# Routed experts: the first gather ahead of the adding products, the first turn of rows inside the second expert's products

## The reference

```
def routed_experts(xt, e_idx, e_w, w_gate, w_up, w_down):
    ...
    def block_ffn(args):
        tok, wt, e = args
        xb = xt[tok]
        hb = jax.nn.silu(xb @ w_gate[e]) * (xb @ w_up[e])
        return (hb @ w_down[e]).astype(F32) * wt[:, None]
    ...
    return jnp.zeros((T, D), F32).at[row_tok].add(yb.reshape(rows, D))
```

## Time and profile before

| | |
|---|---|
| median of 3 runs | 1155.11 us (1152.92 to 1156.42) |
| the profiled execution, its own time | 1163.27 us |
| its span in the trace | 1160.6 us |
| mean granted TensorE clock in it | 0.968 of full |
| PE, DVE, ACT busy | 94%, 73%, 61% of the span |

### The profile page before, as it was taken

One profiled execution on the slowest core, in us unless ns is written; L12 is line 12 of the kernel. 1 busy time (PEld: TensorE's weight loads), 2 busy tenths in 40 slices (PEclk: granted clock), 3 DMA queues, 4 the chain that ended last, 5 costly groups with the idle time before them and its releaser, 6 DMA issues.

```text
span 1160.6 us, 17178 instructions
## 1 busy us (share of the span) xinstructions
PE 1088.2 (94%) x6358; PEld 941.4 (81%) x6358; DVE 843.7 (73%) x1086; ACT 713.5 (61%) x945; POOL 77.3 (7%) x82
## 2 busy tenths in 40 slices
PE   7999969999999999889999999999999878999997
PEld 6877857777877787669988899998788667999996
DVE  5497588999999999567654776667778646767665
ACT  6667359888888887464444555445467545544553
POOL 1001110000000000030000111020000001101100
PEclk9998879999999999889999999999999989999999
DMA  9440518888888888435553554554433223554440
GB/s 372 158 173 4 205 55 326 320 332 328 327 333 324 341 329 330 185 145 182 182 174 117 202 195 154 210 185 154 170 134 120 73 73 131 214 217 181 175 151 36
DMA packets 33605, 232.64 MB, mean 200 GB/s; under 512 B 3856, under 2 KB 3984, under 8 KB 6032
## 3 DMA queue, kind: packets, MB, share of 16 engines
q1 hardware_dynamic: 32688, 229.98, 53.5%
q10 hardware_dynamic: 864, 1.93, 0.5%
HBM read 230.85 MB, written 1.05 MB: 200 GB/s over the span
## 4 chain that ended last, share of the span: by engine, by line
PE 77%; DVE 13%; ACT 6%; issue 3%; POOL 1%; DMA 0%; DVEq 0%; ACTq 0%; POOLq 0%
PE bank L1834 11%; PE bank L1835 11%; PE bank L1836 11%; PE bank L2320 9%; PE bank L2322 9%; PE bank L2321 9%; DVE wlo L1092 5%; PE bank L2189 4%; PE bank L2190 4%; PE bank L2173 2%; ACT whi L512 1%; PE bank L2197 1%; PE bank L2238 1%; PE bank L2237 1%; DVE arena L1482 1%
## 5 line engine op out<-in xcount | busy, mean ns | idle before, releaser
L1092 DVE TENSOR_TENSOR wlo<-raw,whi 128x2048 fp32r<-128x2048 f32 x212 | 482.0, 2287 | 88.6 <-ACT whi L512 87.3
L512 ACT ACTIVATE whi<-raw 128x2048 fp32r<-128x2048 f32 x213 | 406.5, 1917 | 121.9 <-PE bank L2322 65.6
L2320 PE MATMUL bank<-xs,whi 128*128 128x256 f32 x896 | 252.0, 281 | 4.7 <-DVE wlo L1092 3.2
L2321 PE MATMUL bank<-xs,whi 128*128 128x256 f32 x896 | 251.3, 280 | 0.0
L2322 PE MATMUL bank<-xs,wlo 128*128 128x256 f32 x896 | 250.7, 280 | 0.0
L2320 PEld LDWEIGHTS bank<-xs,whi 128*128 128x128 f32 x896 | 169.4, 189 | 6.9 <-DVE wlo L1092 3.6
L2321 PEld LDWEIGHTS bank<-xs,whi 128*128 128x128 f32 x896 | 169.5, 189 | 0.8
L2322 PEld LDWEIGHTS bank<-xs,wlo 128*128 128x128 f32 x896 | 169.4, 189 | 0.0
L1834 PE MATMUL bank<-whi,rounded 128*128 128x512 f32 x344 | 142.2, 413 | 7.4 <-DVE rounded L1491 4.2
L1835 PE MATMUL bank<-wlo,rounded 128*128 128x512 f32 x344 | 139.5, 405 | 0.0
L1836 PE MATMUL bank<-whi,rounded 128*128 128x512 f32 x344 | 139.5, 405 | 0.0
(11 more groups left out here) (319 smaller groups left out, 1475.1 us busy)
## 6 DMA issues: line engine op xcount, KB each, us to landing
raw<-stream SPq DMA_DIRECT2D x215, 1024.0 KB, 4.8
arena<-finals ACTq DMA_DIRECT2D x3, 512.0 KB, 4.3
xres<-x_in SPq DMA_DIRECT2D x2, 512.0 KB, 4.6
raw<-stream SPq DMA_DIRECT2D x4, 256.0 KB, 6.1
out<-xn SPq DMA_DIRECT2D x4, 256.0 KB, 2.1
par<-params SPq DMA_DIRECT2D x1, 844.0 KB, 12.4
cst<-table SPq DMA_DIRECT2D x1, 502.0 KB, 8.9
arena<-p_in ACTq DMA_DIRECT2D x1, 256.0 KB, 5.7
```

Source lines behind the costliest of these rows:

```text
L512: act.activation(whi[:, s, :], raw[:, a, :], ACT.Copy).then_inc(S("high_done"), 1)
L1092: dve.tensor_tensor(wlo[:, s, :], raw[:, unit0 % RAW, :], whi[:, s, :].bitcast(F32), ALU.subtract)\
L2320: pe.matmul(o, whi[:, s, w], xhi[:, kk, :], start=first, stop=False, skip_group_check=True)
L2321: pe.matmul(o, whi[:, s, w], xlo[:, kk, :], start=False, stop=False, skip_group_check=True)
```

## The change

On PE, `fetch(0)` moves in front of `scatter`, with two waits ahead of it: that for `pick_ready`, which stood behind `scatter`, and a new one for the first half of `y_low`, since the gather writes bank 2. `turn_rows(x, 0)` moves from ahead of `pair_gate_up(x, 1)` to between its two units. On ACT, `out(0)` comes ahead of `ahead(4)`, `ahead(5)` ahead of `silu_pair(x, 0)`, `out(2)` ahead of `hidden_high(x, 0)`, and `back_out` goes to the end. On DVE, `pick_quad` and `quad_weights` move from the start of the pair to between `ahead(2)` and `ahead(3)`. No instruction is added or removed but waits.

```
# ACT
                 gate_up_out(x, 0)
+                out(0)
                 ahead(4)
-                out(0)
+                ahead(5)
                 silu_pair(x, 0)
-                ahead(5)
                 gate_up_out(x, 1)
                 out(1)
+                out(2)
                 hidden_high(x, 0)
-                out(2)
                 silu_pair(x, 1)
-                back_out(x)
                 out(3)
                 hidden_high(x, 1)
+                back_out(x)
...
# DVE
-                if not x.second and x.p0 and not x.last_quad:
-
-                    dve.wait_ge(S("slots_turned"), x.count(1))
-                    four = bass.ds(x.quads(1) * 4, 4)
-                    pick_quad(four, 1 - x.buf)
-                    quad_weights(four, 1 - x.buf, S("pick_ready"))
                 ahead(0)
                 ahead(1)
                 if x.p0:
                     y_low(x.count(2, -2))
                 ahead(2)
+                if not x.second and x.p0 and not x.last_quad:
+
+                    dve.wait_ge(S("slots_turned"), x.count(1))
+                    four = bass.ds(x.quads(1) * 4, 4)
+                    pick_quad(four, 1 - x.buf)
+                    quad_weights(four, 1 - x.buf, S("pick_ready"))
                 ahead(3)
...
# PE
                 pair_gate_up(x, 0)
+                if not x.second and not x.last_quad:
+                    pe.wait_ge(S("pick_ready"), x.quads(2))
+                if x.p0:
+
+                    pe.wait_ge(S("y_pair"), x.count(2, -1))
+                fetch(0)
                 if x.p0:
                     scatter(x.count(1))
-                if not x.second and not x.last_quad:
-                    pe.wait_ge(S("pick_ready"), x.quads(2))
-                fetch(0)
-                turn_rows(x, 0)
-                if x.p0:
-                    pe.wait_ge(S("summed"), x.count(2))
-                pair_gate_up(x, 1)
+                    pe.wait_ge(S("summed"), x.count(2))
+                pair_gate_up(x, 1, (0,))
+                turn_rows(x, 0)
+                pair_gate_up(x, 1, (1,))
                 fetch(1)
```

More of the change, by code:

```diff
@@ L1513, in pair_dve @@
                 ahead = (lambda k: split_to(U_MOE + 6 * x.p0 + k)) if x.j is None else (lambda k: split(x.unit(k)))
+                ahead(0)
+                ahead(1)
+                if x.p0:
+                    y_low(x.count(2, -2))
+                ahead(2)
                 if not x.second and x.p0 and not x.last_quad:
@@ L1519, in pair_dve @@
                     quad_weights(four, 1 - x.buf, S("pick_ready"))
-                ahead(0)
-                ahead(1)
-                if x.p0:
-                    y_low(x.count(2, -2))
-                ahead(2)
                 ahead(3)
@@ L2177, in gather, with pair_gate_up @@
                     ins.then_inc(S("gathered"), 1)
-            def pair_gate_up(x, e):
-                for i in range(2):
+            def pair_gate_up(x, e, units=range(2)):
+                for i in units:
                     if x.p0 == 0 and e == 0:
```

## The result

The changed kernel takes 1172.18 us in the median (1171.26 to 1174.32, 4 runs) against 1154.01 (1151.43 to 1156.42, 4 runs): the ratio is 1.016, with a 95% interval of 1.0132 to 1.0189. It is slower by 18 us, where 17.9 were forecast.

What follows compares the result with a forecast made beforehand. PE was taken to bound the expert stage, busy 37.26 of 38.0 us per quad. The terms 12.4 + 8.0 - 0.9 - 1.6 = +17.9 us on the median of 1155.11 gave 1173 us, +1.5%, range 1163 to 1180.

Steps and rivals of the forecast that it cites:

- The gap of 0.72 us at the first units goes: First expert's units on PE, pairs with a pick: 0.72 us less in six pairs, a gain of 4.3 us.
- t0: Start of the last down product of the pair before, from which the prediction counted each pair's times.
- The wait, +12.4 us: PE's gather waits for DVE's late pick, 2.6 us idle; six pairs together become 12.4 us longer.
- the 2.06 of the sum: Net lengthening in us of each pair with a pick, 6.75 - 4.69, with the first units' gain inside.
- The walk from t0: DVE's pick starts at t0 + 5.74, the gather at about t0 + 6.75; PE is there at t0 + 3.97.
- The clock, +8.0 us from five falls of 1.6: Idle 2.6 us ahead of the gather halves PE's clock in five of six pairs, 1.6 us each.
- The turn of rows and the earlier gather: nothing: PE's sum unchanged; DVE's first fold 0.83 us later, inside its 1.00 us idle ahead of the second fold.
- The last quad, -0.9 and -1.6 us: ACT's `gate_up_out` starts 0.45 us earlier in each of two pairs, -0.9; one of two clock falls may stay away, -1.6.
- wait without the clock: Rival: 2.6 us of idle leaves the clock alone, 12.4 - 0.9 - 1.6 = +9.9, 1165 us; chance 0.13.

Runs made afterwards that it cites:

- the filled wait: The changed kernel with 20 added products of 256 columns on PE ahead of the wait for the pick, against the kernel before: 1165.78 us, ratio 1.0077.
- half filled kernel: The changed kernel with 10 added products of 256 columns on PE ahead of the wait for the pick, against the kernel before: 1165.7 us, ratio 1.0091.

## Why the prediction was right

1. *The gap of 0.72 us at the first units goes.* Yes: after, the first units start at t0 + 0.24 (288.16) and 1.86 later (290.02), without a gap, and the gap is back with the pick first.
2. *The wait, +12.4 us.* Measured with the clock kept up, 240.41 - 228.05 = 12.4 us; each of the six pairs is 1.98 to 2.09 us longer, for the 2.06 of the sum. The walk from t0 along ACT, DVE and PE met each start of the pair shown within 0.1 us. Idle times were 2.49 to 2.60 for the 2.6 forecast, 15.2 us for 15.6.
3. *The clock, +8.0 us from five falls of 1.6.* The mechanism holds: filling the wait, wholly or by half, removes all falls. The size was somewhat high. A fall costs about 1.5 us (a pair with one takes 22.77 to 22.95 us, one without 21.4 to 21.5), and the two profiles of the changed kernel have 5 (counting the long one twice) and 3; the stretch of pairs 1 to 13 exceeds that with the filled wait by 247.86 - 240.41 = 7.5 us in one and 244.84 - 240.41 = 4.4 us in the other. By time, the difference of the ratios, 0.83% to 0.72%, is 8 to 10 us; the medians of the changed and the half filled kernel, timed side by side, differ by 6.4.
   Five falls in six rested on six idle times of over 2 us that had all brought one in a single profile. That was too little to go by. In the twelve profiles PE idles 1.88 to 3.64 us ahead of its first product behind the pairs (2.67 in the kernel before); a fall follows in eight of them, once after 1.88 us, and in four none does, once after 3.36 us (the kernel with the pick ahead of `y_low`; the slices are as for the changed kernel run again):

```profile
474.29 0.50 PE L1834 MATMUL bank<-whi,rounded 128*128 128x512 f32 x1 [3.36 <-DVE wlo L1092]
```

```profile
472.00:474.00 2.00, 0.00 (x0) 1.00 0.00 0
474.00:476.00 2.00, 1.71 (x7) 1.00 0.36 66
476.00:478.00 2.00, 2.00 (x14) 1.00 0.88 360
```

   So the length of one idle time does not decide, at these lengths; the share that falls does the pricing, and in the loop it was seven of twelve.
   The Trainium skill (TensorE: Matmul & The Clock Gate, section 'HAM oscillation — how this bites in real kernels') tells of a loop whose wait brings the clock down in every round. Its waits are longer than these, and no run here has such waits in its loop.
4. *The turn of rows and the earlier gather: nothing.* Nearly: with the pick first the pairs have their old lengths, but for the one that waited for a load. DVE's wait for the turned rows divides as expected: there it is 16.6 us in 30 times, where it was 18.6 in 16.
5. *The last quad, -0.9 and -1.6 us.* The order was worth 0.5, not 0.9: `gate_up_out` starts 0.4 us earlier (0.69 for 1.10), but 0.15 us of each pair does not come through. The clock gave up to twice the 1.6: with the new order none of nine profiles has a fall at the last quad's waits (0.69 and 0.65 us); with the old one (1.10 and 0.65 us) all three have one at pair 15's first down product, and the kernel before has one at pair 14's too. That is one or two falls avoided, 1.4 to 2.9 us.

The sum came out to 0.3 us of the measured medians. Its parts were +12.4, +4.4 to 7.5, -0.5 and -1.4 to -2.9, in all 13 to 18; the interval of the ratio is 15 to 22 us. So the closeness of the total is partly luck, that of the wait's term not. The rival 'wait without the clock' is what the two filled kernels are, and it measured 1.0077 and 1.0091, where it was priced at 1.0086 (9.9 of 1155).

Open is why a wait of the same length brings a fall in some rounds and not in others. Not run was the late pick with the early gather alone, without ACT's order and the later turn of rows; that these two have no part in the cost rests on the trace, where the gather waits for the pick's weights and nothing else, and on the walk.

## What to carry to other kernels

Where an instruction moves ahead on one engine and what it waits for moves back on another, walk both engines from one common event to the meeting point: here the late pick alone was free (0.9994), and so was the rest of the change without it (0.9969), but both together cost 1.6%. Look for the place of the producer that is early enough for its consumer and late enough not to hold up the first splits: ahead of `y_low` the pairs with a pick were 0.5 us shorter than before, behind it 0.4, and one split later still they were 2 us longer, and more where the clock fell. A recurring idle time of PE can have a second price, the clock's, and work that covers half of it removed that price wholly here. How often the clock falls cannot be read off a handful of idle times in one profile.

## What the runs showed of the hardware

Useless products made the kernel faster: 10 added products of 256 columns in each of six waits (which left 1.3 to 1.4 us idle of 2.5 to 2.6) took 0.7% off, by keeping the granted clock at 1.00 where it had fallen to 0.50. In the loop idle times of 1.3 to 1.4 us brought no fall in six cases, those of 2.5 to 2.6 us brought seven in twelve. No single length divides the two kinds: in the last quad 1.10 and 0.65 us, 1 us of products apart, brought a fall in four cases of six, 0.69 and 0.65 us in none of eighteen, and 3.36 us behind the pairs once brought none. And a fall can last twice as long (from about 375.7 to 382.6 us) although PE is busy without a break behind the wait.
